# First MLP of a two-layer decoder: squared-ReLU input turned by VectorE and ScalarE in place of TensorE, modulation pieces from a table, row sums on ScalarE

## The reference

```python
c_act = jax.nn.silu(c)
for i in range(DEPTH):                     # DEPTH = 2
    mod = (c_act @ w_ada[i] + b_ada[i])[:, None, :]        # w_ada[i]: 2048 x 12288
    sh_a, sc_a, g_a, sh_m, sc_m, g_m = jnp.split(mod, N_MOD, axis=-1)
    h = x * (1.0 + sc_a) + sh_a
    y = diff_attention(h, ...) if i == 0 else sliding_window_attention(h, ...)
    x = layer_norm(ALPHA * x + (1.0 + g_a) * y, ln_mix_g[i], ln_mix_b[i])
    h = x * (1.0 + sc_m) + sh_m
    y = jnp.square(jax.nn.relu(h @ w_up[i])) @ w_down[i]   # 2048 -> 8192 -> 2048
    x = layer_norm(ALPHA * x + (1.0 + g_m) * y, ln_mlp_g[i], ln_mlp_b[i])
```

## Time and profile before

| | us |
|---|---|
| median of 3 runs | 2228.99 (2226.84 to 2229.18) |
| the profiled execution | 2228.67 |
| its span of instructions | 2226.9 |
| PE busy | 2168.5 (97%) |
| DVE busy | 1790.6 (80%) |
| ACT busy | 981.3 (44%) |

### The profile page before, as it was taken

How to read it: one execution, slowest core, us unless ns; L and a number is a source line. 1 busy time by engine, 2 the same in 40 slices (tenths; PEclk the granted TensorE clock), 3 DMA queues, 4 the chain that set the end, 5 groups by cost and what they waited for, 6 DMA issues and landing times.

```text
span 2226.9 us, 26022 instructions
## 1 busy us (share of the span) xinstructions
PE 2168.5 (97%) x9952; PEld 1791.8 (80%) x9952; DVE 1790.6 (80%) x2057; ACT 981.3 (44%) x1330; POOL 33.4 (2%) x53
## 2 busy tenths in 40 slices
PE   6999999999999999999999999999999999999997
PEld 6887888877888888888888788777888888888886
DVE  6899998887997897888786888777966865874877
ACT  1135444546433443443353655536534443443441
POOL 0001000000000000000000000000000000000000
PEclk9899999999999999999999999999999999999999
DMA  9999888877999999999985643365766676666663
GB/s 360 384 331 347 322 320 300 306 245 256 361 364 325 354 366 335 325 380 350 323 311 190 198 152 119 122 207 190 236 221 223 213 241 206 219 217 219 228 234 113
DMA packets 262592, 596.41 MB, mean 268 GB/s; under 512 B 13426, under 2 KB 14788, under 8 KB 262468
## 3 DMA queue, kind: packets, MB, share of 16 engines
q1 hardware_dynamic: 254800, 579.45, 74.2%
q10 hardware_dynamic: 7668, 15.30, 2.2%
HBM read 592.60 MB, written 2.10 MB: 267 GB/s over the span
## 4 chain that ended last, share of the span: by engine, by line
PE 88%; DVE 7%; DMA 1%; issue 1%; ACT 1%; SPq 0%; DVEq 0%; POOL 0%; ACTq 0%; POOLq 0%
PE pair L1709 25%; PE pair L1711 25%; PE pair L1710 25%; DVE acc L916 2%; DVE w_lo L901 1%; PE pair L1967 1%; PE pair L1969 1%; PE pair L1968 1%; PE pair L1729 1%; PE pair L1731 1%; PE pair L1730 1%; PE turn L2041 1%; DMA y<-in_w_ada_dram 1%; PE turn L2022 1%; PE turn L1603 1%
## 5 line engine op out<-in xcount | busy, mean ns | idle before, releaser
L528 ACT ACTIVATE w_hi<-raw 128x1024 fp32r<-128x1024 f32 x712 | 726.8, 1056 | 620.2 <-PE pair L1711 297.4
L901 DVE TENSOR_TENSOR w_lo<-raw,w_hi 128x1024 fp32r<-128x1024 f32 x712 | 852.5, 1220 | 117.0 <-ACT w_hi L528 110.8
L1709 PE MATMUL pair<-w_hi,h_hi 128*128 128x512 f32 x1456 | 581.3, 399 | 1.5 <-DVE w_lo L901 0.8
L1711 PE MATMUL pair<-w_hi,h_lo 128*128 128x512 f32 x1456 | 567.8, 390 | 0.0
L1710 PE MATMUL pair<-w_lo,h_hi 128*128 128x512 f32 x1456 | 567.3, 390 | 0.0
L1709 PE MATMUL pair<-w_hi,f_hi 128*128 128x512 f32 x1056 | 414.0, 392 | 0.1
L1711 PE MATMUL pair<-w_hi,f_lo 128*128 128x512 f32 x1056 | 411.1, 389 | 0.0
L1710 PE MATMUL pair<-w_lo,f_hi 128*128 128x512 f32 x1056 | 410.9, 389 | 0.0
L929 DVE SCALAR_TENSOR_TENSOR acc<-ada_w,cvec,acc 128x1024 f32<-128x1024 f32 x300 | 383.6, 1279 | 1.8 <-DVE x L1312 0.9
L1709 PEld LDWEIGHTS pair<-w_hi,h_hi 128*128 128x128 f32 x1456 | 273.5, 188 | 62.9 <-DVE w_lo L901 6.3
L1711 PEld LDWEIGHTS pair<-w_hi,h_lo 128*128 128x128 f32 x1456 | 273.2, 188 | 58.4
(11 more groups left out here) (190 smaller groups left out, 1669.5 us busy)
## 6 DMA issues: line engine op xcount, KB each, us to landing
ada_w<-in_w_ada_dram SPq DMA_DIRECT2D x320, 512.0 KB, 6.1
raw<-in_w_up_dram SPq DMA_DIRECT2D x128, 1024.0 KB, 6.1
raw<-in_w_down_dram SPq DMA_DIRECT2D x128, 1024.0 KB, 5.2
raw<-in_a_w_qkv_dram SPq DMA_DIRECT2D x48, 1024.0 KB, 7.6
ada_f<-in_w_ada_dram SPq DMA_DIRECT2D x44, 512.0 KB, 11.5
raw<-in_b_w_qkv_dram SPq DMA_DIRECT2D x20, 1024.0 KB, 5.2
raw<-in_a_w_o_dram SPq DMA_DIRECT2D x16, 1024.0 KB, 6.5
raw<-in_b_w_o_dram SPq DMA_DIRECT2D x16, 1024.0 KB, 5.1
```

The lines of the kernel that those rows point to most:

```text
L528: act.activation(w_hi[:, (b.n * SUB + n) % SPLITS], raw[:, slot, k:k + 2], ACT.Copy).then_inc(hi_ready, 1)
L901: dve.tensor_tensor(w_lo[:, slot, k:k + 2], raw[:, slot, k:k + 2], w_hi[:, (b.n * SUB + n) % SPLITS].bitcast(F32), ALU.subtract).then_inc( ...
L1709: pe.matmul(o, hi[:, kt, at], w[:, k], start=kt == 0, stop=False)
L1711: mm = pe.matmul(o, lo[:, kt, at], w[:, k], start=False, stop=kt == KT - 1)
```

## The change

**1. ON_CHIP takes layer 0 too, in a form of its own (`BY_SCALAR`).** In an up round of the first MLP TensorE's eight transposes go. VectorE, after its third subtile, does one block transpose of 128x1024 from `work` to `turn` (each 32x32 block in its place, `up_turn`); ScalarE then moves the blocks to their quadrants with sixteen copies of 32x256 from `turn` to `work` (`up_move`), eight after its fourth subtile and eight after its fifth, and squares twice after its sixth (`up_square_there`, from `work`). VectorE's `f_lo` follows its own sixth subtile. ScalarE's ReLU stands after its third subtile, not its second.

**2. Pieces by a table.** `MLP_PIECES` gives the number of each round; in the first MLP 192 pieces over 31 rounds. The numbers of the second MLP stay the same.

**3. Row sums on ScalarE.** After `mod_turn` ScalarE copies the eight 128x128 parts of `turn` to scrap with its accumulator on, at its hook 6 (`mod_rows`); VectorE waits for `mod_summed` and adds the bias.

```diff
-ON_CHIP = (1,)
+ON_CHIP = (0, 1)
+BY_SCALAR = (0,)
...
+MLP_ADA = {0: [], 1: [5], 2: [1, 5], 4: [1, 3, 5, 7], 5: [0, 1, 3, 5, 7], 6: [0, 1, 3, 5, 6, 7],
+           7: [0, 1, 3, 4, 5, 6, 7], 8: [0, 1, 2, 3, 4, 5, 6, 7]}
+MLP_PIECES = (4 * [4] + [7, 8, 7, 8] + 2 * (4 * [6] + [7, 8, 8, 8]) + 4 * [6] + 3 * [4],
+              [(i + 1) * 32 // 28 - i * 32 // 28 for i in range(28)] + 3 * [0])
...
+def mlp_sum(layer, b):
+
+    before, after = sum(MLP_PIECES[layer][:b - 1]) // KT, sum(MLP_PIECES[layer][:b]) // KT
+    return before if b > 0 and after > before else None
...
+            def up_move(first, last):
+
+                def run():
+                    act.wait_ge(up_blocks, st.turned.n + 1)
+                    for i in range(first, last):
+                        a, c = i // 4, i % 4
+                        ins = act.activation(by_token(rows32(up_rows(RR), c), a),
+                                             by_feature(rows32(turn[:, 0], a), c), ACT.Copy)
+                    if last == 16:
+                        ins.then_inc(up_moved, 1)
+                return run
...
+            def mod_rows(turned, slot, half):
+
+                def run():
+                    act.wait_ge(t_full[1], turned)
+                    for k in range(8):
+                        col = slot * KT + half * 8 + k
+                        ins = act.activation(sum_junk[:, k], turn[:, 1, span(k * P, P)], ACT.Copy,
+                                             accum_out=mod[:, col:col + 1])
+                    ins.then_inc(mod_summed, 1)
+                return run
...
                     if layer in ON_CHIP:
+                        if i < 4 and layer in BY_SCALAR:
+                            hk[3], hk[4] = up_move(0, 8), up_move(8, 16)
                         if i < 4:
                             hk[5] = up_square_there(i)
                         block_(before=up_relu if i < 4 else None, hooks=hk, at=2)
...
-                    dve.wait_ge(t_full[1], st.t1.at(1))
-                    link(dve.tensor_reduce(at, turn[:, 1].rearrange("p (k s) -> p k s", s=P), AX_X, ALU.add))
+                    st.summed.n += 1
+                    dve.wait_ge(mod_summed, st.summed.n)
                     dve.tensor_tensor(at, at, bvec[:, span(layer * 6 * KT + part * KT + half * 8, 8)],
                                       ALU.add).then_inc(t_free[1], 1)
...
+            def up_turn(b, pp):
+
+                dve.wait_ge(evacuated, b + 3)
+                dve.transpose(turn[:, 0], up_rows(R)).then_inc(up_blocks, 1)
...
                     if layer in ON_CHIP and i < 4:
-                        hooks[3] = up_turn_rest
-                        block_(before=up_turn_across, later=(5, up_rest(i)), ada=mlp_pieces(b, halves), hooks=hooks)
+                        if layer not in BY_SCALAR:
+                            hooks[3] = up_turn_rest
+                        block_(before=up_turn if layer in BY_SCALAR else up_turn_across, later=(5, up_rest(i)), ada=mlp_pieces(layer, b), hooks=hooks)
```

More of the change, by code:

```diff
@@ L57 @@
 MASKED = -1e30
-ON_CHIP = (1,)
+ON_CHIP = (0, 1)
+BY_SCALAR = (0,)
 T0_FIRST = 2
+T1_MLP = 12
 T0_B = T0_FIRST + 16 + (0 if 0 in ON_CHIP else 4 * QUARTERS)
@@ L107, with mlp_pieces @@
 READY = 6
[L110 to L117, removed]
+def mlp_pieces(layer, b):
+    return MLP_ADA[MLP_PIECES[layer][b]]
+def mlp_sum(layer, b):
+    before, after = sum(MLP_PIECES[layer][:b - 1]) // KT, sum(MLP_PIECES[layer][:b]) // KT
+    return before if b > 0 and after > before else None
 class Count:
@@ L140, in __init__ @@
         self.turned = Count()
+        self.summed = Count()
         self.bc = [0, 0]
@@ L208, in trunk @@
         R, RR, SQ = work[:, 0], work[:, 1], work[:, 2]
+        sum_junk = gate[:, 0:ADA_W].rearrange("p (k s) -> p k s", s=P)
         def up_rows(tile):
@@ L331, in trunk @@
         up_moved = sem("up_moved")
+        mod_summed = sem("mod_summed")
         up_hi_ready = sem("up_hi_ready")
@@ L498, in mlp @@
                     src = up(it, i + 1) if i < 3 else down(it, i - 3) if i < 7 else up(it + 1, 0)
-                    load_block(src, mlp_pieces(b, 2 * len(parts)), of)
+                    load_block(src, mlp_pieces(layer, b), of)
             mlp(0)
@@ L801, in mlp @@
                     hk = {6: load_affine(b + 1)} if b in (1, 2) else {}
+                    k = mlp_sum(layer, b)
+                    if k is not None and k < gate_at:
+                        late = hk.get(6)
+                        hk[6] = mod_rows(T1_MLP + k + 1, 4 + k // 2, k % 2)
+                        if late:
+                            hk[7] = late
                     for half in range(2):
-                        if mlp_sum(b + 2, halves) == gate_at + half:
+                        if mlp_sum(layer, b + 2) == gate_at + half:
                             hk[0] = load_gate_bias(layer, 5, half)
@@ L1462, in mlp @@
                     last = it == QUARTERS - 1
-                    k = mlp_sum(b, halves)
+                    k = mlp_sum(layer, b)
                     hooks = {}
@@ L1472, in mlp @@
                     if layer in ON_CHIP and i < 4:
-                        hooks[3] = up_turn_rest
-                        block_(before=up_turn_across, later=(5, up_rest(i)), ada=mlp_pieces(b, halves), hooks=hooks)
+                        if layer not in BY_SCALAR:
+                            hooks[3] = up_turn_rest
+                        block_(before=up_turn if layer in BY_SCALAR else up_turn_across, later=(5, up_rest(i)), ada=mlp_pieces(layer, b), hooks=hooks)
                         continue
                     block_(before=(down_last if last else down_add)(i - 4) if i >= 4 else None,
-                           later=(4, up_lo(i)) if i < 4 else None, ada=mlp_pieces(b, halves), hooks=hooks)
+                           later=(4, up_lo(i)) if i < 4 else None, ada=mlp_pieces(layer, b), hooks=hooks)
             mlp(0, 1, 0)
```

4 lines of the change are left out of this document (1 added, 3 removed).

## The result

| | before | after |
|---|---|---|
| median | 2229.06 us (4 runs) | **2246.88 us** (2244.93 to 2248.89, 4 runs) |
| profiled execution | 2228.67 | 2246.15 |
| its span | 2226.9 | 2244.3 |

The ratio is 1.0086, 95% interval 1.0074 to 1.0098: slower, by 18 us between the medians. (Ratios here are the record's; the two medians alone give 1.0080, and no conclusion hangs on the difference. The experiments ran at three later times, when the kernel before had medians of 2227.41, 2227.96 and 2228.66 us, and each ratio is against the kernel before of its own time.) The forecast had said 2218.5 and faster; the time lies above the range too. It is close to the slower rival's 2243.

What follows compares the result with a forecast made beforehand. TensorE was taken to set the pace, with little room on VectorE. Transposes -14.4, lateness +1.1, round 28 +0.5 and the table's end +2.4 gave -10.4 us, so 2218.5 us; range 2213 to 2236.

Steps and rivals of the forecast that it cites:

- the slower rival: Up rounds of the first MLP: copies don't overlap, cost 0.38 each, VectorE's chain becomes the bound; 2243 us, chance 0.14.
- The bound and the gain: First MLP: TensorE sets the pace; dropping its transposes saves 0.90 us in each of 16 up rounds, -14.4 us.
- The chain's own terms: Up round, ReLU to `f_lo`: block transpose 1.22 us, sixteen copies at 0.28, subtiles 0.97; `f_lo` begins 10.74 after the ReLU.
- the walk: Step-by-step timing of one up round with six pieces, from ReLU through transpose, copies and squares to VectorE's subtile 6.
- Lateness: VectorE falls 0.7 us behind per up round, 0.85 in rounds 0 to 3, catching up in down rounds; stalls 1.1 and 0.5.
- the slack: Up round: VectorE's subtile 6 ends 14.30 us after the ReLU's start against a limit of 15.86, 1.6 us to spare.
- the sum: Whole kernel: -14.4 for transposes, +1.1 and +0.5 for stalls, +2.4 for round 30, together -10.4 us.
- The row sums: After `mod_turn`: eight accumulating ScalarE copies at 0.36, 2.9 us; each such round takes 0.5 us off VectorE's lateness.
- The table's end: Round 30: two pieces before the subtile TensorE awaits cost +2.4 us; its wait becomes 3.8 instead of 1.44.
- The transfers: Rival in down rounds with eight pieces: weight transfers take 23.1 us against 21.76; 2220 to 2229 us, chance 0.14.
- break-even: Up rounds: non-overlapping copies decide where stalls reach 11.5 us, 0.8 us more per round, 0.33 us per copy.

Runs made afterwards that it cites:

- e1: The changed kernel with every second of ScalarE's sixteen copies of an up round left out: 2216.09 us, ratio 0.9948.
- e4: The changed kernel with up-round pieces moved behind VectorE's subtiles 3 and 4, 7 pieces in rounds 24 to 27, none in round 30: 2215.0 us, 0.9941.
- e5: The changed kernel, first eight copies within one quadrant, next eight crossing and unstrided, quadrants kept for four copies (results misplaced): 2223.74 us, one run.
- e6: The changed kernel with only the modulation's row sums put back on VectorE: 2252.45 us, ratio 1.0109.
- e7: The changed kernel with no pieces in round 30 and 7 instead of 6 in rounds 24 to 27: 2242.19 us, ratio 1.0067.
- e2: The changed kernel with the first MLP's transposes given back to TensorE, table and ScalarE row sums kept: 2232.0 us, ratio 1.0018.
- e10: The changed kernel, first eight copies within one quadrant that changes each copy, second eight with changing written quadrant and unstrided source: 2245.86 us, one run.
- e11: e4 with the ScalarE form in the second MLP too, its up-round pieces placed after subtiles 4 and 1: 2208.43 us, ratio 0.9911.
- e9: The changed kernel with its copies reordered so the written quadrant stays for four neighbours and the read one changes: 2248.78 us, ratio 1.0088.

## Why the prediction was wrong, point by point

**The bound and the gain.** Right. TensorE's transposes are worth 14.4 us: e1 shows -14.6 in the up rounds, e4 -14.1, with rounds of 21.76.

**The chain's own terms.** The block transpose was taken at 1.22 and is 1.25 long. The copies are the step that failed: "I take 0.28 and 0.38 as the other end", on the ground that a 256-wide copy steps 0.29. Those rows all start at partition 0; the copies change quadrants and step **0.385**. The same copy as in the earlier trace rows on the upper partitions stepped 0.40 in the same trace. Two batches make 3.08 + 3.13 - 4.48 = 1.73 us more, and the subtile between them steps 1.08 instead of 0.97, another 0.1. Measured from transpose to `f_lo`: 11.57 in nearly every up round, against 9.7 in the walk. (The walk's own terms add up to 0.03 less than the 10.74 it gives, which changes nothing.)

**Lateness.** "0.7 us behind per up round", and 0.85 in the first four rounds, were wrong by that amount. From the transpose of round 8, which has six pieces, to the next VectorE takes 24.37, where the walk had 22.48: 2.6 behind. In round 2 it takes 24.67 where TensorE's work is 21.76: 2.9 behind, the whole of it lost once the slack is used up. VectorE does catch up in the down rounds, as forecast: at the first transpose of each later group it is back at 1.06 after the ReLU. Over all up rounds and round 28 the stalls are 14.9 + 14.4 = 29.3 us, where the sum had 1.6 (1.0 in the first group, 0.1 in the three others, 0.5 in round 28). That is the whole error: 27.7 of 28 us.

**How much of it is the copies.** e5 has copies of 0.295 and still loses 14.4 - 7.6 = 6.8 us of stalls. (Counted against e1, 4.0 of these are in the first group, 0.5 in the two middle ones and 2.4 in the last.) So the remaining 22.5 us hang on the 1.4 us per round by which overlap fails: transpose to `f_lo` takes 10.13 in e5 and 11.57 in the changed kernel. The other 5 us or so are argued, not shown one by one: steps a little longer than in the walk (0.295 on average for 0.28; no overlap at the seams between subtile and copies; 13.10 us behind `f_lo` for the first group, where the walk had 12.9). e5 was run once. The walk had left itself a slack of 1.6 us in a loop that runs four times, and counted each step at its shortest.

**The row sums.** Better than forecast. The first two and the last of the eight, ScalarE in the changed kernel:

```profile
795.85 0.28 ACT L602 ACTIVATE gate<-turn 128x128 f32<-128x128 f32 x1
...
796.11 0.27 ACT L602 ACTIVATE gate<-turn 128x128 f32<-128x128 f32 x1
...
797.61 0.32 ACT L602 ACTIVATE gate<-turn 128x128 f32<-128x128 f32 x1
```

They step 0.25, not 0.36: eight take 2.0 us, not 2.9. The 0.36 came from a pair of exponentials with a bias operand (`exps` in the kernel before), not from copies. Against e6 they save 4.7 us.

**The table's end.** Right: +2.4 forecast, +2.4 measured, and e7 gives it back. The wait forecast as one of 3.8 us came as two, 0.56 and 2.95. (e2, e6 and e10 show 1 to 1.6 us more in the end than the others with the same round 30; why, no run tells.)

**The transfers.** Right that they would not be what limits. Rounds 11 to 15, of which 12 to 15 have 7, 8, 8 and 8 pieces, take 110.62 us in e4 and in e11 between the ReLUs of rounds 11 and 16; before, it was 111.55, with one up round's 0.90 in it.

**The rivals.** The slower one was written down with the mechanism that came true, and its time, 2243, is 4 us from the result: it had 26.5 us of stalls where 29.3 came, and some 7 us for a group where 5.9 to 9.7 came. What was wrong is its chance. Of the two grounds given, "no row has 32 partitions or a strided source" was the better one, and the upper-half rows of L860 in the trace before would have borne it out. Its break-even was 0.33 us per copy; between e5 (0.295, -5.0 in the span) and after (0.385, +17.4) a straight line crosses zero at 0.315, an estimate. The forecast's own figure was 0.035 below that, much less than the 0.10 between the two ends it had named, so 0.14 was far too low.

The estimate from the Trainium skill, "ScalarE: Activation LUTs", *What ACT_TABLE_LOAD costs*, was 0.31 a step. Where the quadrants stay e5 steps 0.27, a little less. The 0.385 of the changed kernel is near what the same section's figures give without the overlap, 0.186 + 0.213 = 0.40, an estimate from that section of the Trainium skill. The rule of the Trainium skill, "VectorE: DVE Perf Modes", *Rules for kernel authors*, which sends a 128x128 transpose to TensorE, names the winner for the changed kernel but not for this work: in e4 and e11 the way without TensorE wins by 12 and 20 us, and the same copies are in all three (4.6 of e11's 20 lie in the second MLP, which was already turned without TensorE).

## What to carry to other kernels

A chain through two engines that recurs in a loop is judged by the loop: time from its start to its end, plus all that its engine does until the next start, against the period of the engine that sets the pace. Before such a chain is costed, each operation's step needs a row that starts at the same partitions, not only one of the same width; where none exists, and the break-even lies between the two ends, the two cases deserve like chances. And where an engine must wait inside such a chain, put its free work into that wait, ahead of what is due after it: moving a few pieces by a subtile or two (e4) was worth more here, 29 us of stalls, than a quarter off every copy (e5), 22.

## What the hardware showed that was not expected

- Eight ScalarE copies of 32x256 take 2.36 us if neighbours read and write the same quadrants and 3.08 if either changes (six forms, e5, e9, e10 and the changed kernel); strides alone and crossing alone don't matter. Within the fast eights the step is 0.27 while the quadrants stay and 0.37 where they change. The seam between a 128-partition subtile and a copy shows the same: 578.78 to 579.86 is 1.08 for an operation of 1.06, where subtile to square steps 0.97. In the trace before, a 64-partition copy between 128-partition operations steps 0.29 and 0.26 on partitions 0 to 63, and 0.40 and 0.41 on 64 to 127.
- A ScalarE copy of 128x128 with its accumulator on steps 0.25 us, less than the 0.36 of the 129-wide exponentials of the earlier trace rows, though each is followed by a read of the accumulator.
